# Half columns in the layer inputs and the gated seams, the lower bounds computed beside the first feed-forward, the second block's projections in four pieces

## What is computed

```python
# first block, layer 0 (gated linear attention + attention) and layer 1 (hgrn), then per layer:
y = mix(rms(x, norm_pre_mix) * (1 + scale) + shift)
x = x + gate * rms(y, norm_post_mix)            # the "gated seam"
y = swiglu(rms(x, norm_pre_ffn) * (1 + scale) + shift)
x = x + gate * rms(y, norm_post_ffn)            # the "gated seam" again
# layer 1's forget gates are bounded below:
lbs = cumsum(softmax(lower_bounds, axis=1), axis=1); lb = lbs[:, layer] - lbs[:, 0]
# second block, per layer:
q, k, v = split(x @ w_qkv)                       # 1024 -> 1536
x = layer_norm(alpha * x + attention(q, k, v) @ w_o)
x = layer_norm(alpha * x + f(x))                 # swiglu in layer 0, 8 experts in layer 1
x = x + (p @ w_ple_proj) * sigmoid(x @ w_ple_gate)   # the "layer input"
```

## Time and profile before

| | us |
|---|---|
| median of 3 runs | 3395.22 |
| lowest, highest | 3392.78, 3396.01 |
| the profiled execution | 3392.76 |
| its span in the trace | 3390.9 |
| PE busy | 3099.5 (91%) |
| DVE busy | 816.0 (24%) |
| ACT busy | 412.2 (12%) |
| POOL busy | 303.7 (9%) |

### The profile page before, as it was taken

One profiled execution on the slowest core, in us unless ns is written; L12 is line 12 of the kernel. 1 busy time (PEld: TensorE's weight loads), 2 busy tenths in 40 slices (PEclk: granted clock), 3 DMA queues, 4 the chain that ended last, 5 costly groups with the idle time before them and its releaser, 6 DMA issues.

```text
span 3390.9 us, 41457 instructions
## 1 busy us (share of the span) xinstructions
PE 3099.5 (91%) x18118; PEld 1769.5 (52%) x18118; DVE 816.0 (24%) x1534; ACT 412.2 (12%) x1006; POOL 303.7 (9%) x359
## 2 busy tenths in 40 slices
PE   6988778999988999899988999877999999999995
PEld 2456544444447777576656766454444434444442
DVE  1146931000036676500132000253000000000003
ACT  1024121000022222200021000121000000000001
POOL 1123710000012233200000000000000000000000
PEclk8989988999999999999989999878999999999997
DMA  8670001212022122244422343304899999999983
GB/s 340 253 259 1 1 0 62 112 64 104 37 59 63 50 56 63 82 155 161 164 74 112 131 180 130 115 26 170 341 407 359 360 387 381 359 363 407 359 323 116
DMA packets 206451, 609.12 MB, mean 180 GB/s; under 512 B 6012, under 2 KB 47196, under 8 KB 199744
## 3 DMA queue, kind: packets, MB, share of 16 engines
q1 hardware_dynamic: 200864, 592.59, 45.9%
q0 software_dynamic: 4944, 13.28, 1.2%
q10 hardware_dynamic: 464, 0.60, 0.1%
HBM read 600.28 MB, written 6.16 MB: 179 GB/s over the span
## 4 chain that ended last, share of the span: by engine, by line
PE 79%; DVE 11%; issue 3%; ACT 3%; DMA 2%; POOL 1%; POOLq 0%; PEld 0%; PEldq 0%; ACTq 0%; SPq 0%; DVEq 0%
PE ps_ffn_gate L590 10%; PE ps_ffn_up L590 10%; PE ps_ffn_down L626 10%; PE ps_moe_down L2938 6%; PE ps_moe_gate L2895 6%; PE ps_moe_up L2895 6%; PE ps_odd L1851 4%; PE ps_lin L1362 4%; PE ps_project L512 3%; PE ps_moe_gate L2900 3%; PE ps_moe_up L2900 3%; PE ps_moe_down L2944 3%; PE ps_lin L296 3%; DVE rec_qd L2130 2%; PE ps_mod L1285 1%
## 5 line engine op out<-in xcount | busy, mean ns | idle before, releaser
L590 PE MATMUL ps_ffn_gate<-hT,ring_buf 128*128 128x256 f32 (+1 forms) x1152 | 342.8, 451 | 4.3 <-issue 2.3
L590 PE MATMUL ps_ffn_up<-hT,ring_buf 128*128 128x256 f32 (+1 forms) x1152 | 336.7, 445 | 1.3
L626 PE MATMUL ps_ffn_down<-ring_buf,ffn_hiddenT 128*128 128x512 f32 x752 | 325.9, 593 | 3.0 <-issue 3.0
L590 PEld LDWEIGHTS ps_ffn_gate<-hT,ring_buf 128*128 128x128 f32 x1152 | 221.6, 193 | 120.0 <-issue 98.7
L590 PEld LDWEIGHTS ps_ffn_up<-hT,ring_buf 128*128 128x128 f32 x1152 | 217.9, 190 | 110.3 <-issue 90.0
L1851 PE MATMUL ps_odd<-ring_buf,hT 128*128 128x256 f32 (+2 forms) x1024 | 236.5, 386 | 9.0 <-ACT hg_kT L1986 5.6
L626 PEld LDWEIGHTS ps_ffn_down<-ring_buf,ffn_hiddenT 128*128 128x128 f32 x752 | 141.7, 190 | 182.0 <-issue 182.0
L671 DVE TENSOR_TENSOR ffn_hiddenT<-ffn_silu_buf,ps_ffn_up 128x256 f32<-128x256 f32 (+1 forms) x72 | 36.2, 503 | 749.8 <-PE ps_ffn_up L590 749.8
L3037 DVE TENSOR_TENSOR moe_hidden_buf<-moe_silu_buf,ps_moe_up 128x768 f32<-128x768 f32 (+1 forms) x32 | 27.3, 854 | 748.4 <-PE ps_moe_up L2900 748.4
L1851 PEld LDWEIGHTS ps_odd<-ring_buf,hT 128*128 128x128 f32 x1024 | 174.6, 193 | 55.8 <-ACT hg_kT L1986 7.0
L2895 PE MATMUL ps_moe_up<-ring_buf,moe_xg_buf 128*64 128x512 f32 (+1 forms) x1024 | 199.5, 542 | 0.0
(11 more groups left out here) (491 smaller groups left out, 3403.7 us busy)
## 6 DMA issues: line engine op xcount, KB each, us to landing
ring_buf<-in_w_exp_up_dram SPq DMA_DIRECT2D x24, 4096.0 KB, 16.6
ring_buf<-in_w_exp_down_dram SPq DMA_DIRECT2D x24, 4096.0 KB, 16.1
moe_third<-in_w_exp_gate_dram SPq DMA_DIRECT2D x16, 4096.0 KB, 17.8
mod_pieces<-in_mod_w_dram SPq DMA_DIRECT2D x40, 1024.0 KB, 6.4
ring_buf<-in_w_exp_gate_dram SPq DMA_DIRECT2D x8, 4096.0 KB, 17.5
ring_buf<-in_odd_w_in_dram SPq DMA_DIRECT2D x40, 512.0 KB, 5.3
moe_third<-in_w_exp_gate_dram SPq DMA_DIRECT2D x8, 2048.0 KB, 10.9
ring_buf<-in_w_exp_up_dram SPq DMA_DIRECT2D x8, 2048.0 KB, 7.8
```

What stands on the lines that cost most here:

```text
L590: mm = nc.tensor.matmul(ps[:, 0:wide], view[:, k, i * P:(i + 1) * P], hT[:, k, first_col:first_col + wide], start=k == 0, stop=k == KD - 1)
L626: mm = nc.tensor.matmul(ps_y[i % 2][:, h, :], hidT[:, b, i * P:(i + 1) * P], view[:, b, h * 512:(h + 1) * 512], start=first, stop=end)
```

## The change

Five edits. (1) `GatedSeam`: the product with the gate row is now an instruction of its own into a new tile `gated`, ahead of the wait for the reciprocal root (where the result lies in PSUM it first waits for the squares); the scaling and the addition to `X` are one instruction for each half of the columns; the second squares, the scaling and the transposes' waits also go by halves. (2) The softmax of the lower bounds moves out of `odd_mixer` to the start of layer 0's feed-forward on POOL, ACT and DVE. (3) In `odd_mixer` head 0 has `lb` as its first step, and DVE does the constants, the four `forget`, then the gain, `silu_q` and `silu_og`. (4) `per_layer_input` has the column half as its outer loop; a gate slot is freed behind the second tile's gate products of that half. ACT, DVE, the transposes and the result's stores (`finish`) follow the same order. (5) `w_qkv` comes in four items of 384 columns, each taken by both tiles. The diff, cut to this (the waits' counts that follow from it are left out):

```diff
-            self.sums = sb(cx, "seam_sums", [P, 2, 4])
+            self.gated = sb(cx, "seam_gated", [P, D])
+            self.sums = sb(cx, "seam_sums", [P, 3, 4])
             self.rstd = sb(cx, "seam_rstd", [P, 2, 4])
 
-        def attach(self, gates, turned, made, room, y_done):
+        def attach(self, gates, turned, made, room, y_done, in_psum=True):
...
             self.y_done(dve, i)
+            if self.in_psum:
+                dve.wait_ge(s_post["post_sums"].handle, s_post["post_sums"].at(i + 1))
+            if i > 0:
+                dve.wait_ge(s_post["post_added"].handle, s_post["post_added"].at(2 * i))
+            link_v(nc.vector.tensor_tensor(self.gated[:, :], self.made(i), self.rows[:, w, :], ALU.mult))
             dve.wait_ge(s_post["post_rstd"].handle, s_post["post_rstd"].at(i + 1))
-            link_v(nc.vector.scalar_tensor_tensor(out=self.room(i), in0=self.made(i), scalar=self.rstd[:, 0, i:i + 1],
-                                                  in1=self.rows[:, w, :], op0=ALU.mult, op1=ALU.mult))
-            nc.vector.tensor_tensor(X[:, t, :], X[:, t, :], self.room(i), ALU.add)\
-                .then_inc(s_post["post_added"].handle, 1)
+            for h in range(2):
+                x = X[:, t, h * 512:(h + 1) * 512]
+                nc.vector.scalar_tensor_tensor(out=x, in0=self.gated[:, h * 512:(h + 1) * 512],
+                                               scalar=self.rstd[:, 0, i:i + 1], in1=x, op0=ALU.mult, op1=ALU.add)\
...
-                    link_g(nc.gpsimd.tensor_scalar(r, self.sums[:, 1, i:i + 1], 1.0, D * EPS_RMS, ALU.mult, ALU.add))
+                    link_g(nc.gpsimd.tensor_scalar(r, self.sums[:, 1, i:i + 1], self.sums[:, 2, i:i + 1],
+                                                   D * EPS_RMS, ALU.add, ALU.add))
                     nc.gpsimd.tensor_tensor(r, r, half_power, ALU.pow).then_inc(s_norm["norm_rstd"].handle, 1)
 
         def act_second(self, act, i):
             if self.following is None:
                 return
-            act.wait_ge(s_post["post_added"].handle, s_post["post_added"].at(i + 1))
             act.wait_ge(s_post["post_sums"].handle, s_post["post_sums"].at(i + 1))
-            nc.scalar.activation(self.junk[:, :], X[:, self.tiles[i], :], ACT.Square,
-                                 accum_out=self.sums[:, 1, i:i + 1]).then_inc(s_norm["norm_sums"].handle, 1)
+            for h in range(2):
+                act.wait_ge(s_post["post_added"].handle, s_post["post_added"].at(2 * i + h + 1))
+                cols = slice(h * 512, (h + 1) * 512)
+                nc.scalar.activation(self.junk[:, cols], X[:, self.tiles[i], cols], ACT.Square,
+                                     accum_out=self.sums[:, 1 + h, i:i + 1]).then_inc(s_norm["norm_sums"].handle, 1)
 
         def dve_second(self, dve, i):
             if self.following is None:
                 return
             dve.wait_ge(s_norm["norm_rstd"].handle, s_norm["norm_rstd"].at(i + 1))
-            nc.vector.tensor_scalar(self.room(i), X[:, self.tiles[i], :], self.rstd[:, 1, i:i + 1], D ** 0.5,
-                                    ALU.mult, ALU.mult).then_inc(s_norm["norm_scaled"].handle, 1)
+            for h in range(2):
+                cols = slice(h * 512, (h + 1) * 512)
+                nc.vector.tensor_scalar(self.room(i)[:, cols], X[:, self.tiles[i], cols], self.rstd[:, 1, i:i + 1],
+                                        D ** 0.5, ALU.mult, ALU.mult).then_inc(s_norm["norm_scaled"].handle, 1)
 
         def pe_turn(self, pe, i):
             src = X[:, self.tiles[i], :] if self.following is None else self.room(i)
-            if self.following is None:
-                pe.wait_ge(s_post["post_added"].handle, s_post["post_added"].at(i + 1))
-            else:
-                pe.wait_ge(s_norm["norm_scaled"].handle, s_norm["norm_scaled"].at(i + 1))
+            ready = s_post["post_added"] if self.following is None else s_norm["norm_scaled"]
             if i >= 2:
                 pe.wait_ge(s_norm["norm_out_v"].handle, s_norm["norm_out_v"].at(i - 1))
                 pe.wait_ge(s_norm["norm_out_a"].handle, s_norm["norm_out_a"].at(i - 1))
             for k in range(KD):
+                if k % (KD // 2) == 0:
...
-                        lambda i: flat_y[i] if resident else Y[:, tiles[i], :], lambda i: Y[:, tiles[i], :], y_done)
+                        lambda i: flat_y[i] if resident else Y[:, tiles[i], :], lambda i: Y[:, tiles[i], :], y_done,
+                        in_psum=resident)
 
...
+                    beside.act_steps(act)
                 for n in range(total):
...
+                    beside.dve_steps(dve)
                 for j in range(chunks):
...
 
-    def odd_mixer(O, bank):
+    class LowerBounds:
+
+
+        def __init__(self, cx):
+            self.lb = sb(cx, "hg_lb", [2, D])
+            self.lb1 = sb(cx, "hg_lb1", [2, D])
+
+        def room(self, cx):
+            self.top = sb(cx, "hg_lb_top", [2, D])
+            self.inv = sb(cx, "hg_lb_inv", [2, D])
+
+        def pool_steps(self, pool):
+            load(pool, "pool", (self.lb[:, :], a["hgrn_lower_bounds"][:, 0, :]),
+                 (self.lb1[:, :], a["hgrn_lower_bounds"][:, 1, :]))
+            pool.sem_inc(loads_ready.handle, 1)
+
+        def act_steps(self, act):
+            nc.scalar.preload_act_table_set("exp_and_others")
+            act.wait_ge(s_odd["bound_ready"].handle, s_odd["bound_ready"].at(1))
+            nc.scalar.activation(self.lb[:, :], self.lb[:, :], ACT.Exp)
+            nc.scalar.activation(self.lb1[:, :], self.lb1[:, :], ACT.Exp).then_inc(s_odd["bound_exp"].handle, 1)
+
+        def dve_steps(self, dve):
+            b0, b1, top, inv = self.lb[:, :], self.lb1[:, :], self.top[:, :], self.inv[:, :]
+            dve.wait_ge(loads_ready.handle, loads_ready.at(1))
+            link_v(nc.vector.tensor_tensor(top, b0, b1, ALU.max))
+            link_v(nc.vector.tensor_tensor(b0, b0, top, ALU.subtract))
+            nc.vector.tensor_tensor(b1, b1, top, ALU.subtract).then_inc(s_odd["bound_ready"].handle, 1)
+            dve.wait_ge(s_odd["bound_exp"].handle, s_odd["bound_exp"].at(1))
+            link_v(nc.vector.tensor_tensor(top, b0, b1, ALU.add))
+            link_v(nc.vector.reciprocal(inv, top))
+            link_v(nc.vector.tensor_tensor(top, b1, inv, ALU.mult))
+            link_v(nc.vector.tensor_tensor(b1, b0, inv, ALU.mult))
+            link_v(nc.vector.tensor_copy(b0, top))
+
...
         TURNED = [("kT", 0), ("fT", 0), ("i", 0), ("i", 1), ("qT", 0), ("ctx", 0), ("rest", 0)]
-        steps = [(0, k, t) for k, t in PROJECTED + [("lb", 0)] + TURNED]
-        for h in range(1, HH):
-            steps += [(h, k, t) for k, t in [("lb", 0)] + PROJECTED + TURNED]
+        steps = [(h, k, t) for h in range(HH) for k, t in [("lb", 0)] + PROJECTED + TURNED]
...
-                load(pool, "pool", (lb[:, :], a["hgrn_lower_bounds"][:, 0, :]),
-                     (lb1[:, :], a["hgrn_lower_bounds"][:, 1, :]))
-                pool.sem_inc(loads_ready.handle, 1)
...
                     if kind == "lb":
...
                 nc.scalar.preload_act_table_set("exp_and_others")
-                act.wait_ge(Z["bound_ready"].handle, Z["bound_ready"].at(1))
-                nc.scalar.activation(lb[:, :], lb[:, :], ACT.Exp)
-                nc.scalar.activation(lb1[:, :], lb1[:, :], ACT.Exp).then_inc(Z["bound_exp"].handle, 1)
-                for kind, t in PROJECTED + [("lb", 0)]:
+                for kind, t in [("lb", 0)] + PROJECTED:
                     take(0, kind, t)
...
             def _(dve):
-                def lower_bounds():
-                    top = masked[0:2, :, :].rearrange("p l n -> p (l n)")
...
 
-                lower_bounds()
-                dve.wait_ge(loads_ready.handle, loads_ready.at(2))
-                link_v(nc.vector.tensor_scalar(gain[:, :], gain[:, :], 0.5, None, ALU.mult))
                 for x in flat:
                     nc.vector.memset(flat[x], 1.0)
                 link_v(nc.vector.memset(total[:, :], 1.0))
                 nc.vector.sem_inc(Z["bound_ready"].handle, 1)
+                for t in range(4):
+                    forget(0, t)
+                dve.wait_ge(loads_ready.handle, loads_ready.at(1))
+                link_v(nc.vector.tensor_scalar(gain[:, :], gain[:, :], 0.5, None, ALU.mult))
                 silu_q(0)
                 silu_og(0)
-                for t in range(4):
-                    forget(0, t)
                 tree(0)
...
-                for i, t in enumerate(tiles):
-                    for h in range(2):
-                        cols = slice(h * 512, (h + 1) * 512)
-                        if i == 0:
-                            await_item(pe, h)
+                for h in range(2):
+                    cols = slice(h * 512, (h + 1) * 512)
+                    await_item(pe, h)
+                    for i, t in enumerate(tiles):
                         view = slot_view(h, KD, 512)
```

(25 more changed lines are left out.)

89 lines of the change are left out of this document (45 added, 44 removed).

## The result

The changed kernel takes 3373.43 us (median of 4 runs, 3372.54 to 3376.57), the kernel before 3394.28 beside it (3392.78 to 3396.01): ratio 0.994, 95% interval 0.9928 to 0.9951, 20.9 us less. The profiled execution took 3372.65 with a span of 3370.8. The forecast was 3376.5, between 3368 and 3385.

A forecast was written before the change was run, and what follows sets the result against it. PE, busy 91% of the span, bounds the kernel, so only its stalls and low-clock stretches can shrink. Terms 7.8 + 2.0 + 6.3 + 6.7 - 4.0 - 0.15 = 18.65 us less gave 3376.5 us as a median, range 3368 to 3385.

The forecast's parts named there:

- The stall in front of the projection: Second block, layer 1's projection: PE's 9.04 us wait for a load shrinks through earlier loads, 7.8 us gained.
- its clock: Layer 1's projection, second block: the clock stays up behind a 1.3 us idle stretch, 2.0 us gained, bounds 0 and 2.0.
- Rival C: The w_qkv load is not early, issued only near 2170: 3381.3 us, or 3386.3 if no sooner at all; chance 0.06.
- Drains: Projections and layer inputs: eight added PE drains at freed items, 0.50 us each, 4.0 us lost, bounds 0 and 6.
- Lower bounds beside the first feed-forward: First feed-forward: the moved softmax lies beside products and costs nothing, paid only above 12 us of lateness.
- The start of the recurrence: Recurrence, head 0: shorter chain to the context keys, 6.3 us gained after two losses, bounds 4.5 and 7.5.
- the 8.0: Recurrence, head 0: context keys 8.6 us behind the last projection's take, like head 1, in place of 16.6.
- the 1.1 lost to POOL's keys: Recurrence, head 0: POOL's keys run beside more of DVE's queries, context keys to state copy 11.7 us against 10.6.
- about half of it comes back: 0.6 lost: Recurrence's start: lb moved in front of the projections costs 1.15 us, about half regained as the clock is low there.
- The seams: Last tiles of four gated seams: 1.9, 1.8 and twice 1.5 us gained, sum 6.7, bounds 3.5 and 8.
- Rival A: Behind layer 1's feed-forward the clock stays up: transposes 1.0, projection 1.6 less, 3373.9 us, about 3371 with half-cost drains; chance 0.14.
- Rival D: Slower: a lower clock in both attention stages, up to 26.1 us, 3402.6; decides from 18.7 us on; chance 0.08 in all.

The follow-up runs named there:

- the first trace: The profiled execution of the changed kernel with all five edits, 3372.65 us.
- the second trace: The changed kernel run once more, nothing altered, beside the kernel with filled seams: median 3374.49 us, ratio 0.994 to the kernel before.
- the part alone: The kernel before with only the lower bounds beside the first feed-forward and the new order of the recurrence's first head: 3391.04 us (0.999).
- the kernel with the product alone: The kernel before with only the gate rows' product done beside the squares, each step on whole columns, not halves: 3391.74 us (0.9989).

## Why the prediction was right, point by point

**The stall in front of the projection (7.8) and its clock (2.0).** As said: 1.20 us left, 7.7 gained, clock 1.00, and the projection 2.2 us shorter before its drains. Rival C (no early load) is out.

**Drains (4.0).** 0.50 each in the projections, as the rows of before gave it. In the layer input it is 0.37 for a drain in the middle; the four cost 1.1 together, not 2.0: that term was 0.9 too large.

**Lower bounds beside the first feed-forward (nothing).** Timeline of after:
```profile
530.16 1.21 DVE L1701 TENSOR_TENSOR hg_lb_top<-hg_lb 2x1024 f32<-2x1024 f32 x1 [7.05 <-POOLq L1690]
...
537.19 6.54 DVE L1706 RECIPROCAL hg_lb_inv<-hg_lb_top 2x1024 f32<-2x1024 f32 x1
...
542.68 7.03 PE L606 MATMUL ps_ffn_gate<-hT,ring_buf 128*128 128x512 f32 x16
...
546.97 0.69 DVE L691 TENSOR_TENSOR ffn_hiddenT<-ffn_silu_buf,ps_ffn_up 128x512 f32<-128x512 f32 x1
549.54 7.03 PE L606 MATMUL ps_ffn_up<-hT,ring_buf 128*128 128x512 f32 x16
```
VectorE waits for POOL's load until 530.16 and comes to the first hidden product 19.6 us behind the first gate product, 3 us later than I had put it. PE's gate and up products stand 6.87 apart without a break, so the cost is nothing, as forecast, and 9 of the 12 us of cover are left.

**The start of the recurrence (6.3).** This term was too large: 4.3 in the first trace, 5.7 in the second, 4.5 with the part alone. In after ScalarE takes the last projection at 1030.13 and the context keys come at 1038.72, 8.6 us in place of 16.6, so the 8.0 is right, and so is the 1.1 lost to POOL's keys (context keys to state copy 11.7 us in place of 10.6). The failed step is "about half of it comes back: 0.6 lost". Timed from the recurrence's start, `lb` in front cost 3.0 us in the first trace and 1.5 in the second: it takes 2.07 us there, and the f products behind it took 17.00 and 15.48, against 15.97 without it. I had put in the 1.15 us of the full clock and halved them; the product in its new place takes 2.07, and what comes back of that, if anything, is less than what one execution differs from the next.

**The seams (6.7).** 6.7, but with other parts. First feed-forward 1.6 in place of 1.9: the first step of the second root takes POOL 0.30, since it adds two sums (0.19 with whole columns), and ScalarE reads its accumulator once more (0.19). The projections gave 1.3 in place of 1.5. Layer 1's gave 2.5 in place of 1.8, the 0.65 being the transposes at the higher clock. The Trainium skill, "VectorE: DVE Perf Modes", section "The TRN2 errata", warned that each more instruction costs a fixed time; here two halves take 1.42 where a whole one takes 1.28 (and from SBUF in the kernel with the product alone), so 0.14, and the trace agrees.

**Rival A** (the shorter gap keeps the clock up) came half true. Behind 2.43 us of idle the transposes ran mostly at the high clock, 0.65 of the 1.0; but the 1.6 in the projection turned into 1.1 lost, since the low stretch began later and lay whole in the projection. In the second trace of the same kernel the transposes took 1.32 again and the projection's first half 12.14 in place of 13.38, so that there the projection gave 0.2 instead: neither trace has the 1.6. The Trainium skill, "TensorE: Matmul & The Clock Gate", Part 1, says that a cold start's length varies from run to run; the trace agrees (17.00 and 15.48 us for the same products of the same kernel).

**Rival D** (the attentions' clock turns against it) didn't come in the first trace: layer 0's is as long as before, layer 1's 1.0 shorter. But its mechanism exists, at a size far under the 18.7 us that it needed: in the second trace of the same kernel layer 0's attention is 2.2 us longer (0.75 in place of 0.82), and one stage later it shows at 2 to 3 us in five of fourteen traces.

So 16.7 of the 18.7 come from the steps that were named, and 3.5 more from stages that nobody edited. The 3.5 are luck and not the forecast's: in the second trace of the changed kernel the named steps give 19.6, and the stages without an edit are 3.6 longer than before, not shorter. On the mean of the two traces the named steps are right to 0.5 us; each by itself is off by 1 to 2 us, mostly where the clock is low. For the profiled execution that gives 3372.65 where 3374.1 was forecast (2.0 too much in the terms, 3.5 from outside them); the other 1.6 of the 3.1 by which the median lies lower come from how the profiled executions stand to their medians.

## What to carry to other kernels

Where the busiest engine waits at a seam, price the wait twice: its length, and what the next products lose at the lower clock; filling the wait with products whose result nobody reads gave back 10.7 us here, more than all edits of the seams (6.7); a fill must begin inside the wait, or it is paid in full (19.5 us). A load issued as soon as its slot could be free was worth nearly its whole stall here (7.7 of 9.0 us), even at the price of a few drains. Judge an edit of 1 to 3 us by its own rows, and run the same kernel twice before you read a difference of two traces.

## What the runs showed of the hardware

- Eight transposes take 1.04 us at the high clock and 1.94 to 1.97 at the low one; in a row of identity transposes one takes 0.113 us (46 in 5.21), less than the 0.13 that I had counted.
- The same 64 records (32 products) in an unedited stage take 27.73 or 29.7 to 30.5 us, by how the clock stands at their start. What decides it is open: the attention in front ends at 0.50 or at 0.60 to 0.87 with PE as busy in either.
- Transposes of the identity alone bring the clock up (of 200 in a row behind 22.39 us of idle time the first 4 us ran at 0.50, the next 4 at 0.97, the rest at 1.00), and 46 of them kept it at 1.00 through a wait of 6.5 us.
- A 3 MB load issued 23 us ahead and a 1.5 MB one leave the same wait (1.22 and 1.20 us).
- The opening, with no edit in any kernel, ended between 454.7 and 460.5 us in the traces. Stages were therefore compared by their own length.
